# Turning packed key and query tiles by a rounded product in place of a 32-bit transpose, in a hybrid convolution and attention layer

## The reference

```python
h = rmsnorm(x, g_mix)                       # x: (T, 1024)
proj = h @ w_in                             # 1024 -> 2560 columns
a, gate, q, k, v = split(proj, [512, 1024, 1536, 2048])
u = a * sigmoid(gate)                       # GLU, then causal depthwise conv, width 31
c = silu(layernorm(dwconv(u) + b_dw)) @ w_pw
q = rmsnorm(q.reshape(T, 8, 64), g_q)       # per head
k = rmsnorm(k.reshape(T, 8, 64), g_k)
z = q @ k.T / 8                             # per head
l = where(mask, log_sigmoid(-z), 0)
A = where(mask, exp(log_sigmoid(z) + reverse_cumsum(l) - l), 0)
o = A @ v
x = x + concat(c, o) @ w_out
x = x + relu(rmsnorm(x, g_ff) @ w_ff1)**2 @ w_ff2
return x, k, v, last_30_rows_of_u
```

## Time and profile before

| | us |
|---|---|
| median of 3 executions | 3094.45 |
| lowest, highest | 3091.27, 3097.13 |
| the profiled execution | 3089.33 |
| its span, first to last instruction | 3087.5 |
| TensorE matmuls busy | 2774.3 |
| VectorE busy | 1719.1 |
| ScalarE busy | 1008.2 |
| GpSimd busy | 753.0 |

### The profile page before, as it was taken

How to read it: one execution, slowest core, us unless ns; L and a number is a source line. 1 busy time by engine, 2 the same in 40 slices (tenths; PEclk the granted TensorE clock), 3 DMA queues, 4 the chain that set the end, 5 groups by cost and what they waited for, 6 DMA issues and landing times. The chain is left out here.

```text
span 3087.5 us, 37298 instructions
## 1 busy us (share of the span) xinstructions
PE 2774.3 (90%) x13936; PEld 2304.8 (75%) x13936; DVE 1719.1 (56%) x2617; ACT 1008.2 (33%) x2017; POOL 753.0 (24%) x622
## 2 busy tenths in 40 slices
PE   5679766798999989899999989899999999999999
PEld 4556555677778777778888878677778777888887
DVE  4686663655667246646777436753778862322222
ACT  4222432234555112124554221222555540211110
POOL 4431332444555102102222002200333320000000
PEclk9789878899999999899999999899999999999999
DMA  8277457567676855656554653674444347344342
GB/s 308 102 259 268 145 183 256 218 242 259 235 258 230 309 202 190 216 180 245 185 181 161 251 205 134 201 253 180 152 161 158 110 163 287 154 173 155 149 179 86
DMA packets 262047, 616.19 MB, mean 200 GB/s; under 512 B 23217, under 2 KB 159409, under 8 KB 213741
## 3 DMA queue, kind: packets, MB, share of 16 engines
q1 hardware_dynamic: 261869, 613.80, 55.8%
HBM read 444.79 MB, written 168.94 MB: 199 GB/s over the span
## 5 line engine op out<-in xcount | busy, mean ns | idle before, releaser
L1081 POOL TENSOR_TENSOR beta<-beta,stay 128x512 f32<-128x512 f32 (+3 forms) x328 | 324.5, 992 | 769.6 <-DVE stay L1722 769.6
L1862 PE MATMUL ps<-h2T_hi,w_s 128*128 128x512 f32 (+1 forms) x1280 | 467.5, 365 | 15.3 <-ACT kqT L1252 7.9
L2152 PE MATMUL ps<-w_s,hid_hi 128*128 128x512 f32 (+1 forms) x1088 | 437.0, 402 | 20.9 <-DVE hid_lo L1796 20.9
L1863 PE MATMUL ps<-h2T_lo,w_s 128*128 128x512 f32 (+1 forms) x1280 | 455.4, 356 | 0.0
L1864 PE MATMUL ps<-h2T_hi,w_s 128*128 128x512 f32 (+1 forms) x1280 | 455.3, 356 | 0.0
L2153 PE MATMUL ps<-w_s,hid_lo 128*128 128x512 f32 (+1 forms) x1088 | 426.1, 392 | 0.0
L2154 PE MATMUL ps<-w_s,hid_hi 128*128 128x512 f32 (+1 forms) x1088 | 425.8, 391 | 0.0
L1352 ACT ACTIVATE stay<-ps 128x512 f32<-128x512 f32 (+3 forms) x328 | 173.5, 529 | 495.9 <-DVE ps L1710 272.5
L994 POOL TENSOR_TENSOR w_s<-w_raw,w_s 128x1024 fp32r<-128x1024 f32 x94 | 244.7, 2623 | 327.1 <-ACT w_s L1138 327.1
L1791 DVE TENSOR_TENSOR resid<-ps,resid 128x512 f32<-128x512 f32 x256 | 176.1, 688 | 258.2 <-PE ps L2154 257.7
L1526 DVE SCALAR_TENSOR_TENSOR cacc<-uT,vecs,cacc 128x512 f32<-128x512 f32 (+1 forms) x360 | 288.5, 857 | 1.5
(11 more groups left out here) (195 smaller groups left out, 4963.0 us busy)
## 6 DMA issues: line engine op xcount, KB each, us to landing
w_s<-w_scratch SPq DMA_DIRECT2D x282, 1024.0 KB, 7.7
w_scratch<-w_s SPq DMA_DIRECT2D x94, 1024.0 KB, 8.0
w_raw<-in_w_ff SPq DMA_DIRECT2D x64, 512.0 KB, 5.0
a_k<-k_scratch SPq DMA_DIRECT2D x80, 256.0 KB, 4.1
a_v<-v_scratch SPq DMA_DIRECT2D x80, 256.0 KB, 3.9
a_q<-q_scratch SPq DMA_DIRECT2D x64, 256.0 KB, 4.7
w_raw<-in_w_in SPq DMA_DIRECT2D x20, 512.0 KB, 7.4
mix_scratch<-ohl SPq DMA_DIRECT2D x66, 128.0 KB, 2.8
```

The source lines that it names most:

```text
L1081: nc.gpsimd.tensor_tensor(v[0:q.r, 0:n], v[0:q.r, 0:n], stay[q.z % 3][0:q.r, 1:n + 1], ALU.mult).then_inc(s_a, 1)
L1862: nc.tensor.matmul(out, w[0], x[0], start=start, stop=False)
L1863: nc.tensor.matmul(out, w[0], x[1], start=False, stop=False)
L2152: nc.tensor.matmul(o, hid_hi[x][:, k, q0:q0 + r], wh[:, c0:c0 + BANK], start=k == 0, stop=False)
```

## The change

A second identity `ident_r` of the rounded type is placed in on-chip memory; ScalarE fills it with a copy of `ident` after its first four squares, and increments `vec_ok`. The waits for `vec_ok` at the first GLU go from 2 to 3. In `turn_packed` the call of `transpose`, with both operands seen as 32-bit floats, becomes a plain matmul of the packed tile, in its rounded type, and the rounded identity. Bank, columns, order, waits and increments of the turns stay.

```diff
@@ on-chip memory
         ident = place("ident", [P, P])
+        ident_r = place("ident_r", [P, P], F32R)
@@ scalar, gate
                 if u == 0:
-                    act.wait_ge(vec_ok, 2)
+                    act.wait_ge(vec_ok, 3)
@@ scalar, start
             for i in range(4):
                 norm_squares(0, 0, i)
+            nc.scalar.copy(ident_r[:], ident[:]).then_inc(vec_ok, 1)
             act.wait_ge(vec_t, 1)
@@ vector, ag
                         if m == 0:
-                            dve.wait_ge(vec_ok, 2)
+                            dve.wait_ge(vec_ok, 3)
@@ tensor, ag
                 if c == 0:
-                    pe.wait_ge(vec_ok, 2)
+                    pe.wait_ge(vec_ok, 3)
@@ tensor, turn_packed
                 for k in range(4):
-                    ins = nc.tensor.transpose(ps[:, bank, k * r:(k + 1) * r],
-                                              packed[0:r, m % 2, 4 * q + k, :].bitcast(F32), ident[0:r, 0:r])
+                    ins = nc.tensor.matmul(ps[:, bank, k * r:(k + 1) * r], packed[0:r, m % 2, 4 * q + k, :],
+                                           ident_r[0:r, 0:r], start=True, stop=True)
                 ins.then_inc(kqT_ps, 1)
```

## The result

| | before | after |
|---|---|---|
| median of 20 executions, us | 3092.45 | 3101.74 |
| lowest, highest, us | 3089.11, 3098.15 | 3095.04, 3106.16 |
| ratio, with 95% interval | | 1.0026 [1.0019, 1.0033] |
| span of the profiled execution, us | 3087.5 | 3099.0 |
| mean granted clock of TensorE, profiled execution | 0.955 | 0.951 |

The change made the kernel 0.26% slower, 9.3 us by the medians. That lies in the predicted range, but it is not the forecast: the likeliest case was no change that can be measured, + 1.1 us. It is the first rival, the clock held less, which had 20%; a slower kernel had 0.15. That the time fell into the range doesn't make the forecast right.

A forecast was written before the change was run, and what follows sets the result against it. The kernel was taken as a TensorE stream with short gaps, 90% busy. Full turns + 0.4 us after covered ones and narrow turns + 0.7, all else 0, gave + 1.1 us: 3095.6 us on the median, range 3087 to 3103.

The forecast's parts named there:

- the likeliest case: Whole kernel: + 1.1 us, 3095.6 us on the median; with the case that nothing changes in kind, 66%.
- the first rival, the clock held less: Turn groups between waits in the projections: products hold TensorE's clock less than transposes, 3102 to 3104 us; chance 20%.
- The full turns, + 0.5 us: 256 full turns in TensorE's stream: 0.113 us each as products against 0.111, + 0.5 us, some 0.4 after covered turns.
- the rival of the hidden loads (3084): Products in series hide their weight loads and start 0.06 us apart: - 10 us, 3084 us; chance 7%.
- The narrow turns, + 0.7 us: 16 turns of the 64 running frames: 0.113 us each against 0.07, + 0.7 us, ends 0 and 1.4.
- The added copy and the raised waits, nothing: ScalarE's identity copy, about 0.27 us, fits its 9.10 us idle gap; waits raised to 3 before the first GLU add nothing.
- The waits for ScalarE: 18 turns waited 45.5 us for ScalarE's copy kqT, L1252; claimed to stay near 45 us.
- The clock, "I take it as equal, 0 us": TensorE's granted clock in gaps of the projections: products count as activity as much as transposes do, 0 us.
- The rival's sum: Clock held less: 1.6 us per place that loses the clock, none hidden; with + 1.1, four to five places give 3102 to 3104.
- The clock sooner: Behind turns at the low clock, products would start at the high clock: 16 us at most, half taken, 3087 us; chance 7%.

## Why the prediction was right and where it was wrong

*The full turns, + 0.5 us:* right. 0.112 each in the stream against 0.111, and 1.97 us for eight at the low clock in both. The products come as far apart as the loads of the earlier trace rows, 0.114, and the rival of the hidden loads (3084) is out.

*The narrow turns, + 0.7 us:* right in size, within the ends 0 and 1.4. Their loads, of chunk 3 (timeline of PEld; part of it at the low clock), took 1.23 us for eight where four took 0.32 in the earlier trace rows; busy time went up by 1.0 us.

```profile
1948.28 1.23 PEld L1935 LDWEIGHTS ps<-ident_r,packed 64*128 64x128 f32 x8 [2.10 <-ACT kqT L1253]
```

*The added copy and the raised waits, nothing:* right. The copy took 0.28 us in ScalarE's gap, and vecs came 0.13 us earlier than in the earlier trace rows, not later; the run with the copy alone is at 0.9998.

```profile
10.50 0.28 ACT L1459 CAST ident_r<-ident 128x128 fp32r<-128x128 f32 x1
19.47 0.27 ACT L1461 COPY vecs<-ps 128x136 f32<-128x136 f32 x1 [8.69 <-PE ps L2199]
```

*The waits for ScalarE:* right, 44.9 us against 45.5.

*The clock, "I take it as equal, 0 us":* this is the step that failed. The argument ahead of it was sound: turns do count. It should have been carried one line further. The 0.06 us between two matmuls of 128 columns and the 0.111 between turns were both in the rows, and I used them as a reason for the rival and not for the forecast. Equal pace isn't equal activity. The run with two short idle matmuls shows that more loads don't make up for it (0.61 behind the wait), and the run with 256 columns shows that more moved columns do (1.00).

Why the transpose counts for more is an inference. Eight products of the 32-bit ones with 512 columns take 3.44 us at 2047 us, 0.43 each, where rounded ones take 0.226. If a 32-bit transpose moves its columns at that slower pace, its 128 take 0.43 / 4 = 0.11 us, which is its whole slot, while a rounded product's take half of that. No run shows this by itself; the traces show its effect.

*The rival's sum:* its price per place was 1.6 us, and 1.66 was measured between groups. It named 162, 204, 1206, 1911 and 1921 us. New falls are at 162, 171, 1206, 1215 and 1939; behind 1921 the clock was low before too, and now longer, for + 1.7 us (group to group 9.78 us before, 11.52 after); 1911 didn't change. At 204 the turns ran at the high clock after the change and the products behind them at the low one, which nearly cancels: 7.56 us from the group's start to that of its last product before, 7.84 after. The places at 171 and 1215 I had left out, though they repeat the ones before them.
That the rival's sum, + 7.5 to + 9.1 us for four to five places, comes so near to the 9.3 measured is partly luck. It takes it that none of a place's price is hidden. In the profiled pair the 3.3 us of chunk 0 were made up before chunk 2, 1.67 of them in the wait at 204; chunk 2 kept 3.3 and chunk 3 about 3.5, and 2.35 us came at 1390, where the copy-only run with transposes has the low clock as well. How these parts fall out in the other executions isn't known, so the clock as the cause is shown, but not the sum by places.

*The clock sooner* (3087), which the rule of the Trainium skill (TensorE: Matmul & The Clock Gate, "Part 4: PE-mode transpose") would give, is out: the stretch from 221.90 to 228.70 is still at 0.50 after the change. By that rule products in place of transposes can't lose the clock; here they lost it, 0.955 to 0.951, and lost 0.0026 of the time with it.

## What to carry to other kernels

Two forms of an instruction with the same pace can differ in what they keep busy; where TensorE idles between short bursts, compare the granted clock behind each wait before calling an exchange free, and compare starts farther down to see whether the loss stays. If the clock falls at a wait whose length something else sets, matmuls that compute nothing, of many columns and into a free bank, are worth trying in it, as many as the wait holds and none where there is no wait: here six were worth 0.35% over the kernel before; that leaving out those without a wait gave 0.1% of it isn't shown, since the intervals overlap. And where a loss of 0.26% shows in no group of instructions, the distance between two groups that wait for the same thing points at it.

## What the runs showed of the hardware

- With 128 columns and at the high clock, a plain product of 32-bit operands is two matmuls in the trace, 0.112 us each; a transpose of a 32-bit tile is one, 0.111; a rounded product is one, 0.112.
- Ahead of groups of eight rounded products, two matmuls with 512 moved columns in the wait kept the clock at 1.00 behind it, two with 128 didn't (0.61), with the same number of loads.
- Behind the same wait of 1.68 us, eight products with six of them moving 256 columns kept it at 1.00, eight with 128 each didn't (0.59).
- Transposes of 32-bit tiles held TensorE's clock where rounded products that take as long didn't: 1.00 against 0.59 to 0.66 behind waits of 1.68 us.
